# Expert stage of two fused transformer blocks: a pair's down products behind the next pair's gates and ups, and a finer, k-wise release of the first weight buffers

## What is computed

```
(silu(xb @ w_gate[e]) * (xb @ w_up[e])) @ w_down[e]      # 1024 -> 256 -> 1024
```

## Time and profile before

| what | value |
|---|---|
| median of 3 runs | 1308.89 us (1308.36 to 1309.65) |
| span of the profiled execution | 1307.5 us |
| busy share of PE / ACT / DVE / POOL over the span | 97% / 35% / 46% / 41% |
| the expert stage, from its first gate product to the last row of the output | 1059.3 to 1307.5 us |

### The profile page before, as it was taken

The page is one execution under the profiler, slowest core; times in us unless marked ns, Lnnn a source line. Parts: engine busy times, 40 slices in busy tenths (PEclk is TensorE's granted clock), DMA queues, the critical chain, the costliest instruction groups (busy, mean ns, idle before and its releaser), DMA issues.

```text
span 1307.5 us, 17452 instructions
## 1 busy us (share of the span) xinstructions
PE 1264.9 (97%) x6158; PEld 940.9 (72%) x6158; DVE 605.1 (46%) x1126; ACT 460.4 (35%) x770; POOL 532.0 (41%) x681
## 2 busy tenths in 40 slices
PE   8999999999999999999999999999999988999887
PEld 7767777788888888888888788777888863333333
DVE  4868768625442422222226765757152362222215
ACT  5557543435444333133244524165222201010102
POOL 4644323235555645545455665335554111111100
PEclk9999999999999999999999999999999999999999
DMA  7422212112334433434333333312429979999996
GB/s 225 102 65 65 66 49 65 50 54 76 112 96 113 128 97 93 133 98 129 98 95 114 89 105 81 81 48 66 129 64 349 357 271 409 424 425 424 424 425 260
DMA packets 211576, 214.26 MB, mean 164 GB/s; under 512 B 31499, under 2 KB 193021, under 8 KB 199348
## 3 DMA queue, kind: packets, MB, share of 16 engines
q1 hardware_dynamic: 202960, 203.40, 45.8%
q0 software_dynamic: 4752, 8.10, 1.7%
q10 hardware_dynamic: 3796, 1.86, 0.5%
HBM read 205.76 MB, written 16.78 MB: 170 GB/s over the span
## 4 chain that ended last, share of the span: by engine, by line
issue 38%; POOL 31%; PE 26%; DMA 1%; ACT 1%; DVE 1%; POOLq 0%; SPq 0%; DVEq 0%; ACTq 0%
POOL wlo L628 31%; PE bank L2152 8%; PE bank L2169 4%; PE bank L1787 3%; PE bank L1789 3%; PE bank L1788 3%; PE side L1817 1%; ACT hid L1050 1%; DMA y<-y_rows 1%; DVE hid L1620 1%; PE bank L2191 1%; PE bank L1828 1%; PE side L1789 1%; PE side L1788 1%; PE side L1787 1%
## 5 line engine op out<-in xcount | busy, mean ns | idle before, releaser
L628 POOL TENSOR_TENSOR wlo<-raw,whi 128x256 fp32r<-128x256 f32 x644 | 498.3, 805 | 523.5 <-ACT whi L732 523.3
L1788 PE MATMUL bank<-actB_lo,whi 128*128 128x512 f32 x608 | 236.7, 389 | 0.0
L1787 PE MATMUL bank<-actB_hi,whi 128*128 128x512 f32 x576 | 227.6, 395 | 0.5 <-POOL wlo L628 0.5
L1789 PE MATMUL bank<-actB_hi,wlo 128*128 128x512 f32 x576 | 224.4, 390 | 0.0
L732 ACT ACTIVATE whi<-raw 128x1024 fp32r<-128x1024 f32 x161 | 169.0, 1051 | 151.8 <-PE bank L1789 124.9
L1787 PE MATMUL bank<-actA_hi,whi 128*128 128x512 f32 x400 | 157.3, 393 | 0.6 <-DVE actA_lo L1141 0.6
L1789 PE MATMUL bank<-actA_hi,wlo 128*128 128x512 f32 x400 | 156.2, 390 | 0.0
L1788 PE MATMUL bank<-actA_lo,whi 128*128 128x512 f32 x400 | 156.2, 390 | 0.0
L1788 PEld LDWEIGHTS bank<-actB_lo,whi 128*128 128x128 f32 x608 | 114.2, 188 | 24.0 <-issue 1.0
L1787 PEld LDWEIGHTS bank<-actB_hi,whi 128*128 128x128 f32 x576 | 108.2, 188 | 25.8 <-issue 2.3
L1789 PEld LDWEIGHTS bank<-actB_hi,wlo 128*128 128x128 f32 x576 | 108.1, 188 | 22.7
(11 more groups left out here) (401 smaller groups left out, 1668.4 us busy)
## 6 DMA issues: line engine op xcount, KB each, us to landing
dn<-in_w_exp_down SPq DMA_DIRECT2D x33, 1024.0 KB, 17.7
gu<-in_w_exp_gate SPq DMA_DIRECT2D x31, 1024.0 KB, 16.8
gu<-in_w_exp_up SPq DMA_DIRECT2D x31, 1024.0 KB, 19.7
raw<-in_w_in SPq DMA_DIRECT2D x57, 512.0 KB, 3.9
raw<-in_w_up SPq DMA_DIRECT2D x32, 512.0 KB, 3.9
raw<-in_w_down SPq DMA_DIRECT2D x32, 512.0 KB, 3.8
raw<-in_w_out SPq DMA_DIRECT2D x16, 512.0 KB, 3.9
raw<-in_w_in SPq DMA_DIRECT2D x16, 256.0 KB, 3.1
```

The lines of the kernel that those rows point to most:

```text
L628: ins = nc.gpsimd.tensor_tensor(wlo[:, slot, at], raw[:, slot, at], whi[:, slot, at].bitcast(F32), ALU.subtract)
L1787: mm(b[:, :], w_hi, hi[:, k, :], start=first, stop=False)
L1788: mm(b[:, :], w_hi, lo[:, k, :], start=False, stop=False)
L1789: ins = mm(b[:, :], w_lo, hi[:, k, :], start=False, stop=last)
```

## The change

On TensorE the gates and ups of unit q + 1 are issued before the hidden of q is turned and before the downs of q; the rows of q + 2 are turned between the two. ACT and DVE follow: silu of q + 1 before the copy of q; rows of q + 2, hidden of q + 1, then y of q. Unit 0 uses the common `gate_up` with matmuls of 512 columns. Unit 0's buffers are freed in three pieces along k (0 to 1, 2 to 3, 4 to 7, gates and ups together) and unit 1's in two (0 to 3, 4 to 7); each piece is refilled at once, and SP then issues the downs of unit 4, and from unit 5 on gates and ups ahead of downs.

```diff
-QUARTERS_E = [(g, slice(k, k + 4)) for g in range(2) for k in (0, 4)]
+EARLY_PIECES = ((slice(0, 2), slice(2, 4), slice(4, 8)), (slice(0, 4), slice(4, 8)))
...
-    return 32 * (n // GU_BUFS + 1) + (32 if n >= GU_BUFS and n % GU_BUFS < 2 else 0)
+    first = n % GU_BUFS // 2
+    pieces = len(EARLY_PIECES[first]) if n >= GU_BUFS and first < len(EARLY_PIECES) else 1
+    return 32 * (n // GU_BUFS + pieces)
...
-            for i, (g, ks) in enumerate(QUARTERS_E):
-                if i < len(QUARTERS_E) - 1:
-                    sp.wait_ge(S("first_used"), i + 1)
-                else:
-                    sp.wait_ge(S("gate_up_done"), 1)
-                for n in places_of(GU_BUFS // 2):
-                    e = expert_at(n)
-                    sp.dma_start(gu[n % GU_BUFS][:, g, ks, :].rearrange("p j n -> p (j n)"),
-                                 (wg_v, wu_v)[g][:, e, ks.start * DE:ks.stop * DE])\
-                        .then_inc(S(f"gu_in{n % GU_BUFS}"), 16)
-            for q in range(GU_BUFS // 2 + 1, EXTRA_AT + 1):
-                for n in places_of(q):
-                    sp.wait_ge(S("down_done"), unit_of(n - D_BUFS) + 1)
-                    down(n)
-                for n in places_of(q):
-                    sp.wait_ge(S("gate_up_done"), unit_of(n - GU_BUFS) + 1)
-                    gate_up(n)
-            for q in range(EXTRA_AT + 1, UNITS_E):
+            used = 0
+            for early, pieces in enumerate(EARLY_PIECES):
+                for ks in pieces:
+                    if ks.stop < NK:
+                        used += 1
+                        sp.wait_ge(S("first_used"), used)
+                    else:
+                        sp.wait_ge(S("gate_up_done"), early + 1)
+                    for n in places_of(GU_BUFS // 2 + early):
+                        e = expert_at(n)
+                        for g, w_v in enumerate((wg_v, wu_v)):
+                            sp.dma_start(gu[n % GU_BUFS][:, g, ks, :].rearrange("p j n -> p (j n)"),
+                                         w_v[:, e, ks.start * DE:ks.stop * DE]).then_inc(S(f"gu_in{n % GU_BUFS}"), 16)
+            for n in places_of(D_BUFS // 2):
+                sp.wait_ge(S("down_done"), unit_of(n - D_BUFS) + 1)
+                down(n)
+            for q in range(D_BUFS // 2 + 1, UNITS_E):
...
+            silu(0)
             for q in range(LAST_E):
-                if q == EXTRA_AT:
+                if q + 1 == EXTRA_AT:
                     act.wait_ge(S("over_listed"), 1)
-                silu_and_turned(q)
+                if q + 1 < LAST_E:
+                    silu(q + 1)
+                turned_hidden(q)
...
             rows_turned(0, 1)
             place_overflow()
+            rows_turned(1, 2)
+            hidden_of(0)
             over = None
             for q in range(LAST_E):
-                hidden(q % 2, slotv[:, 0, column(q):column(q) + 1], q + 1)
-                rows_turned((q + 1) % 2, q + 2)
+                if q + 2 < UNITS_E:
+                    rows_turned(q % 2, q + 3)
+                if q + 1 < LAST_E:
+                    hidden_of(q + 1)
                 if q == 0:
                     list_overflow()
                 y_of(q)
...
+                    if k + 1 < NK and k + 1 in [ks.stop for ks in pieces]:
+                        ins.then_inc(S("first_used"), 1)
                 ins.then_inc(S("gate_up_done"), 1)
...
             turn_rows_of(0)
+            gate_up_of(0)
+            turn_rows_of(1)
             for q in range(LAST_E):
-                gate_up_of(q)
-                turn_rows_of(q + 1)
+                if q + 1 < LAST_E:
+                    gate_up_of(q + 1)
                 if q == 0:
...
                 turn_hidden(q % 2, q + 1)
+                if q + 2 < UNITS_E:
+                    turn_rows_of(q + 2)
                 down_of(q)
```

More of the change, by code:

```diff
@@ L1041, in _, with silu @@
             over = None
-            def silu_and_turned(q):
+            def silu(q):
                 j, p = q % 2, column(q)
@@ L1051, in silu_and_turned, with turned_hidden @@
                   ACT.Silu, scale=slotv[:, 0, p:p + 1]).then_inc(S("silu_made"), 1)
+            def turned_hidden(q):
                 act.wait_ge(S("hid_turned"), q + 1)
-                a(hidT[:, j, :], side[2][:, 0:DE], ACT.Copy).then_inc(S("hid_t_made"), 1)
+                a(hidT[:, q % 2, :], side[2][:, 0:DE], ACT.Copy).then_inc(S("hid_t_made"), 1)
+            silu(0)
             for q in range(LAST_E):
-                if q == EXTRA_AT:
+                if q + 1 == EXTRA_AT:
                     act.wait_ge(S("over_listed"), 1)
-                silu_and_turned(q)
+                if q + 1 < LAST_E:
+                    silu(q + 1)
+                turned_hidden(q)
                 if q == EXTRA_AT:
@@ L1072, in _ @@
             for_overflow(act, over, overflow)
-            silu_and_turned(LAST_E)
+            silu(LAST_E)
+            turned_hidden(LAST_E)
             nc.scalar.preload_act_table_set("natural_log_exp_and_others")
@@ L1678, in y_of, with hidden_of @@
                       S(f"scattered{q % 2}") if q >= 2 else None, 16 * (q // 2))
+            def hidden_of(q):
+                hidden(q % 2, slotv[:, 0, column(q):column(q) + 1], q + 1)
             rows_turned(0, 1)
             place_overflow()
+            rows_turned(1, 2)
+            hidden_of(0)
             over = None
             for q in range(LAST_E):
-                hidden(q % 2, slotv[:, 0, column(q):column(q) + 1], q + 1)
-                rows_turned((q + 1) % 2, q + 2)
+                if q + 2 < UNITS_E:
+                    rows_turned(q % 2, q + 3)
+                if q + 1 < LAST_E:
+                    hidden_of(q + 1)
                 if q == 0:
@@ L2144, in turn_rows, with gate_up @@
                         ins.then_inc(S("xe_used"), 1)
-            def gate_up(j, weights, rows_made):
+            def gate_up(j, weights, rows_made, pieces=()):
                 for k in range(NK):
@@ L2181, in down_of @@
                 down(q % 2, [dn[n % D_BUFS] for n in places_of(q)], q + 1, q if q else None)
[L2183 to L2193, removed]
             def gate_up_of(q):
-                if q == 0:
-                    first_gate_up()
-                    return
                 for n in places_of(q):
                     pe.wait_ge(S(f"gu_in{n % GU_BUFS}"), gu_landings(n))
-                gate_up(q % 2, [gu[n % GU_BUFS] for n in places_of(q)], 2 * q + 2)
+                gate_up(q % 2, [gu[n % GU_BUFS] for n in places_of(q)], 2 * q + 2,
+                        EARLY_PIECES[q] if q < len(EARLY_PIECES) else ())
             over = None
```

## The result

The changed kernel takes 1315.16 us (median of 4 runs, 1313.62 to 1315.29), the kernel before, run beside it, 1309.27 (1308.36 to 1309.85). The ratio is 1.0044, interval 1.0032 to 1.0056: 5.8 us slower (5.9 by the medians), between 4.2 and 7.4. The direction was forecast, the size was not: +3.1 was said, and the median lies just above the range. The profiled execution was the fastest of the four (1313.62, span 1311.7).

The account below looks back on a forecast made before the run. The prediction took the expert stage to be bound by its weight transfers. End 3.7, less 1.4 for the earlier landing, plus 0.8 for the clock gave +3.1 us: median 1312.0, range 1308.4 to 1315.0.

Parts of the forecast that it names:

- Rival (b): Expert stage: TensorE's chain is the bound after all; 11 us faster, 1298; chance 0.05.
- The start of the stage: Early expert stage: idle DMA time won back; with a scatter issued later, unit 15's weights land 1.4 us earlier.
- second thin spot: DMA queue after 1082 us, before unit 5's gates are issued: thin again, 0.5 us given back (bounds 0 and 1.6).
- The end of the stage: After unit 15's gates: unit 14's downs and the shared banks come first; 3.5 to 4.1 us later, 3.7 taken.
- TensorE's branch: From unit 15's downs through unit 16's products to y2: costs 4.1 less 0.62 of slack, 3.5 us.
- the slack of 0.62: Kernel before: TensorE finished unit 16's gates and ups and found y2 0.62 us late.
- The scatter's branch: From unit 15's downs through its scatter to y2's loads: costs 4.1 us less 0 to 1.6 saved by the scatter.
- The clock: Unit 15's gates: TensorE's clock may halve after an idle wait; 0.8 us taken, bounds 0 and 1.7.
- Rival (d): Before unit 15: the clock falls for certain, else as forecast; +4.0 us, 1312.9; chance 0.46 together with the forecast.
- rival (c): Early stage: thin queue costs more, last weights 1.2 us later, and the clock falls; +6.6 us, 1315.5; chance 0.09.
- (f): Early stage: transfers in pieces never run full, staying at 292 GB/s; +9.8 us, 1318.7; chance 0.03.
- (e): Expert units: gathers come late because rows of q + 2 are turned soon after their issue; chance under 0.02.

Follow-up runs that it names:

- e3: Changed kernel's order of products alone, with quarters of unit 0's buffers and SP's order as in the kernel before; 1323.78 us, ratio 1.0105.
- e9: The changed kernel unaltered, measured again; 1311.93 us, ratio 1.0034 to the kernel before.
- e1: Changed kernel with ten dummy matmuls keeping TensorE busy ahead of the weight waits of units 13, 14 and 15; 1312.98 us, ratio 1.0029.
- e10: Changed kernel with unit 0's buffers freed and refilled in four quarters as before, unit 1's in two pieces; 1312.57 us, ratio 1.0034.
- e11: Changed kernel with quarters for unit 0 and, from unit 9 on, the old order of products; 1306.35 us, ratio 0.9995 to the kernel before.
- e5: Kernel before with only unit 15's gates and ups put ahead of unit 14's hidden and downs; 1314.73 us, ratio 1.0038.
- e12: As e11, with four dummy matmuls ahead of the waits of units 14 and 15; 1307.00 us, ratio 0.9997 to the kernel before.
- e2: Changed kernel with unit 14's downs back ahead of unit 15's gates and ups; 1310.29 us, ratio 1.0009 to the kernel before.
- e7: Changed kernel up to unit 8, old order of products from unit 9 on; 1308.91 us, ratio 1.0004 to the kernel before.
- e4: Changed kernel's pieces and SP order alone, with the old order of products; 1312.10 us, ratio 1.0020 to the kernel before.
- e8: As e7, with eight dummy matmuls ahead of the waits of units 13, 14 and 15; 1309.92 us, ratio 1.0006 to the kernel before.

## Why the prediction was right or wrong

**What bounds the kernel: right.** 424 GB/s stays, e3 shows that TensorE's shorter chain is worth nothing when the queue runs dry. Rival (b), TensorE as the bound, is refuted. The bytes moved early say when the last weights land. Here they are counted from 3 us after unit 0's gates over 27 us (12 and 15 us at their mean rates); the shift that follows from them at 424 GB/s is an estimate. The measured shift is that of unit 15's gates, counted from unit 0's, in the profiles in which unit 15 waited:

| run | MB in 27 us | estimated shift, us | measured shift, us |
|---|---|---|---|
| before | 9.17 | 0 | 0 |
| changed | 9.99 | -1.9 | -2.55 |
| e9 | 10.22 | -2.5 | -2.6 |
| e1 | 9.64 | -1.1 | -1.7 |
| e10 | 9.86 | -1.6 | -1.6 |
| e11 | 10.14 | -2.3 | -2.4 |
| e5 | 9.25 | -0.2 | -0.2 |
| e3 | 6.12 | +7.2 | +7.3 |

**The start of the stage: right in mechanism.** Forecast: unit 15's gates 1.4 us earlier. Measured: 2.55 in the profile, counted from unit 0's gates, of which up to 1.2 is unit 0's own luck with the clock (7.61 against 8.78); e1, with 8.52 there, has them 200.8 us after unit 0's gates, 1.7 earlier than before. The 0.5 for a second thin spot was not there. The bound of 1.2 us later does not follow from the terms: with the 1.6 and the 2.2 that the prediction itself names, they reach 2.2 later.

**The end of the stage: right in mechanism, a little too dear.** Forecast 10.4 us from the gates' end to the downs' end, measured 10.15. Forecast 3.5 to 4.1 for the whole end, 3.7 taken; measured 3.85 - 0.6 = 3.25. TensorE's branch decided, and the slack of 0.62 came back as read. The scatter's branch fell out of the chain: issued at 1281.72, with y2's loads at 1284.52, the scatter of unit 15 took 2.8 us, against 5.5 before. That saves 2.7, where up to 1.6 was allowed for. No weights went beside it (62 GB/s in those 2.8 us); no run separates that from other reasons.

```profile
1281.72 0.97 POOL L650 DMA_INDIRECT y_rows<-ye,tabi  x1 [4.25 <-DVE ye L1637]
...
1284.52 2.24 SPq L614 DMA_DIRECT2D y<-y_rows  x4
```

**The clock: here the prediction failed.** The step was "In the new order each late unit waits 14.8 - 12.15 = 2.7 us or more without any work", then "A fall costs 1.7 us of the gates and ups that follow" and "I take half, 0.8 (bounds 0 and 1.7)". Three things in it were wrong. The wait was 4.32, not about 2.7. TensorE's own work between the last two landings was as forecast, 7.09 + 1.25 + 0.15 + 3.65 = 12.14, but from one landing to the next passed 16.46 us, not 14.8: the 14.8 left out gathers and scatters, and two scatters and a gather were issued beside the weights there (6.98 MB by the queues' bytes, against 6.35 in the kernel before between its last two landings, 14.92 us apart). After 4.3 us without work the low clock did not end after 3.3 us as at the stage's start: it covered 5.8 us of work, so it cost 2.9. And it was no even chance: in both profiles of the changed kernel the same four of the last six units were hit (10, 12, 13 and 15), while unit 14, after 2.05 us, ran at full clock (7.09), which left unit 15 the long wait. The upper bound of the term was taken from one row, and that row's fall was a short one. With 2.9 in place of 0.8 the same sum gives +5.2, 1314.1, inside the interval of the result. That it comes so near is partly luck: the start gained more than forecast and the end cost less, so the three terms as measured give -2.55 + 2.9 + 3.25 = +3.6, and with the 0.6 ahead of the stage the +4.2 of the profile. Rival (d), a fall for certain, was the nearest in mechanism (+4.0). The 1315.5 of rival (c) lies nearer in number, but by accident: its thin queue did not come, nor did (f); and no wait for a gather (e) stands in the chain.

**The profiled execution and the median** differ by 1.5 us in the changed kernel. The profile shows no more than that its start was a good one; what the three others had more is not seen. The profiled execution, 1313.62, lies inside the forecast range; the median is out of it by 0.2 us, and for that the clock's 2.9 us and this open 1.5 are both needed.

**The Trainium skill** (DMA: Bandwidth & Descriptors, section Bandwidth) wants transfers of at least 1 MiB. By its figure for a lone 1 MB the pieces would have been bound to 341 GB/s; the stretch 1075 to 1082 of the changed kernel, mostly pieces of 512 KB with several in flight, ran at 417. In the thin first 12 us all rates but one (354, e11) stayed below 341, with 512 KB pieces as with 256 KB ones; but these 12 us hold time in which little had been issued, so they are no test of it.

**Wait for weights ahead of a unit's gates, and what the gates took**, from the profiles of the study (7.09 us is full clock):

| wait, us | gates, us |
|---|---|
| 1.1 to 2.34 (more than fifteen cases) | 7.09 to 7.10, but for one: 8.77 (1.98 in e12, behind 1.1 us of busy-work) |
| 2.5 to 3.1 | 7.09 to 7.10 (2.78 in e2; 2.96 in e1; 3.08 in e11 and e12) or 8.46 to 8.80 (2.50 in e1, 2.57 in e3, 2.78 in e9, 2.82 changed, 3.04 in e7 and e10, 3.06 in e4, 3.07 in e7, 3.09 in e8) |
| 3.2 to 4.2 | 8.4 to 8.8 (eleven cases, as 3.25 and 4.18 changed, 3.74 in e2), or 9.87 and 10.02 (3.32 in e2, 3.61 in e3) |
| 4.3 to 4.5 | 10.01 (changed, e9), 10.04 (e3), 9.79 (e10), once 8.78 (4.48 in e3) |
| 6.7 | 10.05 (e5) |

The length of the wait alone does not fix the cost; it shifts the odds from nothing to 1.7 and then 2.9 us. A wait of 2.78 us was followed by 7.09 us in e2 and by 8.78 in e9.

## What to carry to other kernels

When a stage is bound by transfers, a tighter order on TensorE moves no bytes sooner except where it frees a buffer while the queue is thin; look for those stretches, they are all that it can win. A software pipeline has to be closed before the last transfer lands: whatever still stands behind the last unit's first product (here one unit's downs and a shared pair of banks, 3.9 us) is paid, less the slack that stood there: 3.3 of the 3.9 us reached the end. Every microsecond that TensorE saves in such a stage turns into idle time in front of the critical product, and may come back at half clock; allow for more than the shortest fall that the trace shows when the wait is longer than the one ahead of it.

## What was not expected of the hardware

A wait of 4.3 us cost unit 15's gates 2.9 us in both profiles of the changed kernel, waits of 2 to 4.2 us anything between nothing and 2.9, and one of 6.7 us no more than 2.9. The same unit 0 took 7.1, 7.6 or 8.8 us from one execution to the next, by where its low clock lay. The rate of a thin queue varied widely between executions with the same early order, 242 to 324 GB/s over the same 12 us. And in the first 20 us of the stage busy DMA engines did not mean full speed: at a DMA share of 1.01 to 1.03 stretches of 5 us ran at 356 (e2), 379 (changed) and 382 GB/s (e1) with 256 KB pieces about, but also at 367 (e10, 1075 to 1080) and 374 (e11, 1070 to 1075) with quarters; later the same share gave 424.
